# Latent attention's order rewritten on TensorE, ScalarE and VectorE

## What is computed

```python
h = xn @ w_down                                     # 1024 -> 256 + 128 + 32
c_q, c_kv, k_r = jnp.split(h, [256, 384], axis=-1)
q = (rms_norm(c_q, q_norm_g) @ w_uq).reshape(b, s, 16, 96)
q_n, q_r = q[..., :64], q[..., 64:]                 # q_r and k_r are rotated
kv = (rms_norm(c_kv, kv_norm_g) @ w_ukv).reshape(b, s, 16, 128)
k_n, v = kv[..., :64], kv[..., 64:]
logits = (q_n . k_n + q_r . k_r) * 96 ** -0.5
p = softmax(logits)
o = p . v
h = h + o @ w_out                                   # 1024 -> 1024
```

## Times and profile before

| | us |
|---|---|
| median of 3 runs | 1656.93 (1654.86 to 1660.21) |
| the profiled execution's own time | 1659.3 |
| its span | 1657.3 |
| TensorE busy in the span | 1632.1 (98%) |
| VectorE / ScalarE busy | 1050.7 (63%) / 852.4 (51%) |

### The profile page before, as it was taken

How to read it: one execution, slowest core, us unless ns; L and a number is a source line. 1 busy time by engine, 2 the same in 40 slices (tenths; PEclk the granted TensorE clock), 3 DMA queues, 4 the chain that set the end, 5 groups by cost and what they waited for, 6 DMA issues and landing times.

```text
span 1657.3 us, 24225 instructions
## 1 busy us (share of the span) xinstructions
PE 1632.1 (98%) x9542; PEld 1401.4 (85%) x9542; DVE 1050.7 (63%) x1197; ACT 852.4 (51%) x1078; POOL 51.1 (3%) x51
## 2 busy tenths in 40 slices
PE   8999999999999999999999999999999999999999
PEld 7878888757888888888897888888889999888887
DVE  6766565766665676667676666676667444566665
ACT  5654444665444464445675544564445444554443
POOL 2000000000000040000010000000000000000000
PEclk9999999989999999999999999999999999999999
DMA  9535554323554455554443555554545444445540
GB/s 368 193 126 194 200 202 181 124 89 111 220 203 181 180 189 200 188 192 157 148 166 141 208 183 195 184 201 183 202 178 192 176 154 166 166 153 203 203 177 26
DMA packets 42717, 294.24 MB, mean 178 GB/s; under 512 B 4736, under 2 KB 5040, under 8 KB 8592
## 3 DMA queue, kind: packets, MB, share of 16 engines
q1 hardware_dynamic: 39168, 281.04, 46.5%
q0 software_dynamic: 2752, 10.58, 1.8%
q10 hardware_dynamic: 720, 1.51, 0.2%
HBM read 289.96 MB, written 3.15 MB: 177 GB/s over the span
## 4 chain that ended last, share of the span: by engine, by line
PE 88%; DVE 6%; ACT 3%; issue 2%; DMA 1%; SPq 0%; DVEq 0%; ACTq 0%
PE ups L270 26%; PE accs L249 14%; PE accs L251 13%; PE accs L250 13%; PE ups L268 11%; DVE wlo L243 2%; PE ups L273 2%; ACT whi L239 1%; DVE h L652 1%; DMA raw<-weights 1%; PE ups L405 1%; PE ups L402 1%; PE ups L407 1%; PE ups L2290 1%; PE ups L448 1%
## 5 line engine op out<-in xcount | busy, mean ns | idle before, releaser
L243 DVE TENSOR_TENSOR wlo<-raw,whi 128x2048 fp32r<-128x2048 f32 x265 | 609.0, 2300 | 229.1 <-ACT whi L239 229.0
L270 PE MATMUL ups<-xhl,whi 128*128 128x512 f32 x1824 | 634.2, 396 | 0.0
L239 ACT CAST whi<-raw 128x2048 fp32r<-128x2048 f32 x265 | 505.2, 1909 | 79.2 <-PE accs L251 78.9
L268 PE MATMUL ups<-xhl,wlo 128*128 128x256 f32 x1596 | 445.0, 279 | 0.0
L270 PEld LDWEIGHTS ups<-xhl,whi 128*128 128x128 f32 x1824 | 331.0, 188 | 64.2
L268 PEld LDWEIGHTS ups<-xhl,wlo 128*128 128x128 f32 x1596 | 300.9, 189 | 10.1
L249 PE MATMUL accs<-whi,hidh 128*128 128x512 f32 x692 | 272.1, 393 | 0.0
L251 PE MATMUL accs<-whi,hidl 128*128 128x512 f32 x692 | 269.7, 390 | 0.0
L250 PE MATMUL accs<-wlo,hidh 128*128 128x512 f32 x692 | 269.5, 390 | 0.0
L249 PE MATMUL accs<-whi,xhl 128*128 128x256 f32 (+1 forms) x576 | 177.6, 308 | 1.6 <-DVE xhl L2140 1.6
L251 PE MATMUL accs<-whi,xhl 128*128 128x256 f32 (+1 forms) x576 | 172.1, 299 | 0.0
(11 more groups left out here) (263 smaller groups left out, 1614.1 us busy)
## 6 DMA issues: line engine op xcount, KB each, us to landing
raw<-weights SPq DMA_DIRECT2D x265, 1024.0 KB, 4.8
gain<-gains POOLq DMA_DIRECT2D x9, 512.0 KB, 3.8
rel_scratch<-sub_rstd POOLq DMA_DIRECT2D x1, 2048.0 KB, 17.4
big<-rel_scratch POOLq DMA_DIRECT2D x1, 1536.0 KB, 8.5
h<-x_in SPq DMA_DIRECT2D x2, 512.0 KB, 6.7
raw<-weights SPq DMA_DIRECT2D x2, 512.0 KB, 10.1
tabs<-consts POOLq DMA_DIRECT2D x1, 1024.0 KB, 7.2
gain<-gains ACTq DMA_DIRECT2D x1, 512.0 KB, 5.1
```

What stands on the lines that cost most here:

```text
L239: nc.scalar.copy(whi[:, m % SPLIT, :], raw[:, m % RAW, :]).then_inc(hi_ready, 1)
L243: nc.vector.tensor_tensor(wlo[:, m % SPLIT, :], raw[:, m % RAW, :], whi[:, m % SPLIT, :].bitcast(F32), ALU.subtract).then_inc(lo_ready, 1)
L268: nc.tensor.matmul(bank[:, 0:T], W(wlo, n, k, j * P, (j + 1) * P), xh[:, k, :], start=False, stop=False)
L270: mm = nc.tensor.matmul(bank, W(whi, n, k, j * P, (j + 1) * P), xhl[:, :, k, :], start=k == 0, stop=k == KC - 1)
```

## The change

The lists of the three engines are rewritten for the pairs of latent attention. No arithmetic, tile or transfer is added or dropped.

- TensorE: `vals(1, 0)` moves ahead of `scores(0)`, `keys(2)` and `vals(0, 1)` ahead of `turn(0)`, and so every later weight piece comes earlier; output pieces start in the fifth pair's round (behind `turn(7)`) where they began behind `turn(9)`. Of the third output slab three pieces run around `turn(15)` and `values(7)`, and `last_slabs` is entered with `begun=True`, behind them. Banks and counts are adapted (`c_taken` 7 for the second rotation).
- ScalarE: the split of `n_c + 4` runs ahead of `exps(0)`. The four splits of output slabs each come behind `turned_copy(2c)`: the first in pair 3, the others in pairs 4, 5 and 6.
- VectorE: `split_low` runs only behind `back(2c+1)`: for `n_co` in pair 3 (behind `back(7)`), and for the others in pairs 5, 6 and 7. `v_copy(0, 1)` runs behind `back(3)`.

The diff, cut to its core (every changed line; unchanged lines left out):

```diff
@@ -299,12 +299,15 @@
-def last_slabs(pe, n, f0, f1, q, ready=None):
-    pe.wait_ge(lo_ready, n + 1)
-    project_out(n, *f0, blocks=(0,))
-    project_out(n, *f0, blocks=(1,), halves=(0,))
+def last_slabs(pe, n, f0, f1, q, ready=None, between=None, begun=False):
+    if not begun:
+        pe.wait_ge(lo_ready, n + 1)
+        project_out(n, *f0, blocks=(0,))
+        if between:
+            between()
+        project_out(n, *f0, blocks=(1,), halves=(0,))
     pe.wait_ge(lo_ready, n + 2)
@@ -1309,7 +1312,7 @@
...
     def query_turn(s, bank):
-        pe.wait_ge(S("c_taken"), (1, 6)[s])
+        pe.wait_ge(S("c_taken"), (1, 7)[s])
         nc.tensor.matmul(bank, rotc, q_ropes, start=True, stop=True).then_inc(S("c_qrot"), 1)
@@ -1371,81 +1374,87 @@
...
     vals(0, 0, accs[:, 2, :]).then_inc(S("c_q"), 1)
+    pe.wait_ge(S("c_taken"), 2)
+    vals(1, 0, accs[:, 3, :]).then_inc(S("c_q"), 1)
     pe.wait_ge(S("c_taken"), 3)
...
     scores(0)
-    vals(1, 0, accs[:, 3, :]).then_inc(S("c_q"), 1)
     pe.wait_ge(S("c_taken"), 4)
     keys(1, accs[:, 0, :]).then_inc(S("c_q"), 1)
+    keys(2, accs[:, 1, :]).then_inc(S("c_q"), 1)
+    pe.wait_ge(S("c_v"), 1)
+    vals(0, 1, accs[:, 2, :]).then_inc(S("c_q"), 1)
     turn(0)
...
     pe.wait_ge(lo_ready, n_c + 5)
-    queries(4, 2, accs[:, 1, :]).then_inc(S("c_q"), 1)
     pe.wait_ge(S("c_v"), 2)
+    queries(4, 2, accs[:, 3, :]).then_inc(S("c_q"), 1)
     values(0)
-    queries(4, 0, accs[:, 2, :]).then_inc(S("c_q"), 1)
+    pe.wait_ge(S("c_taken"), 5)
+    queries(4, 0, accs[:, 0, :]).then_inc(S("c_q"), 1)
     turn(2)
-    pe.wait_ge(S("c_taken"), 5)
     scores(2)
     turn(3)
-    keys(2, accs[:, 3, :]).then_inc(S("c_q"), 1)
+    pe.wait_ge(S("c_v"), 3)
+    keys(3, accs[:, 2, :]).then_inc(S("c_q"), 1)
     values(1)
-    query_turn(1, accs[:, 0, :])
+    query_turn(1, accs[:, 1, :])
     turn(4)
...
     turn(5)
-    keys(3, accs[:, 1, :]).then_inc(S("c_q"), 1)
+    vals(1, 1, accs[:, 3, :]).then_inc(slab_used, 1)
     values(2)
-    pe.wait_ge(S("c_taken"), 7)
-    vals(0, 1, accs[:, 2, :]).then_inc(S("c_q"), 1)
+    pe.wait_ge(S("c_taken"), 8)
+    queries(4, 1, accs[:, 0, :]).then_inc(slab_used, 1)
     turn(6)
-    pe.wait_ge(S("c_taken"), 8)
     pe.wait_ge(S("c_qrope"), 2)
...
     turn(7)
-    vals(1, 1, accs[:, 3, :]).then_inc(slab_used, 1)
+    pe.wait_ge(lo_ready, n_co + 1)
+    pe.wait_ge(S("c_taken"), 10)
+    pe.wait_ge(S("att_o_low"), C_BASE // 2 + 2)
+    out_piece(0, 0, 0)
     values(3)
-    queries(4, 1, accs[:, 0, :]).then_inc(slab_used, 1)
+    out_piece(0, 0, 1)
     turn(8)
...
     turn(9)
-    pe.wait_ge(S("c_taken"), 10)
-    pe.wait_ge(lo_ready, n_co + 1)
-    pe.wait_ge(S("att_o_low"), C_BASE // 2 + 2)
-    out_piece(0, 0, 0)
     pe.wait_ge(S("c_v"), 4)
+    out_piece(0, 1, 0)
     values(4)
-    out_piece(0, 0, 1)
+    out_piece(0, 1, 1).then_inc(slab_used, 1)
     turn(10)
...
     turn(11)
-    out_piece(0, 1, 0)
-    values(5)
-    out_piece(0, 1, 1).then_inc(slab_used, 1)
-    turn(12)
-    scores(7)
-    turn(13)
     pe.wait_ge(lo_ready, n_co + 2)
...
     out_piece(1, 0, 0)
+    values(5)
     out_piece(1, 0, 1)
+    turn(12)
+    scores(7)
+    turn(13)
+    out_piece(1, 1, 0)
     values(6)
+    out_piece(1, 1, 1).then_inc(slab_used, 1)
     turn(14)
-    out_piece(1, 1, 0)
+    pe.wait_ge(lo_ready, n_co + 3)
+    pe.wait_ge(S("att_o_low"), C_BASE // 2 + 6)
+    out_piece(2, 0, 0)
     turn(15)
-    out_piece(1, 1, 1).then_inc(slab_used, 1)
+    out_piece(2, 0, 1)
     values(7)
-    pe.wait_ge(S("att_o_low"), C_BASE // 2 + 6)
-    last_slabs(pe, n_co + 2, features(4), features(6), 3,
+    out_piece(2, 1, 0)
+    last_slabs(pe, n_co + 2, features(4), features(6), 3, begun=True,
                ready=lambda: pe.wait_ge(S("att_o_low"), C_BASE // 2 + 8))
@@ -1518,69 +1527,51 @@
...
     heads(qc, 2, accs[:, 0, :])
+    split_high(act, n_c + 4)
     exps(0)
     exps(1)
-    split_high(act, n_c + 4)
-    turned_copy(0)
...
     heads(kc, 2, accs[:, 0, :])
+    turned_copy(0)
...
     act.wait_ge(S("c_q"), 7)
+    heads(kc, 4, accs[:, 1, :])
+    o_high(0)
+    act.wait_ge(S("c_q"), 9)
     act.wait_ge(S("c_qrope"), 1)
-    ropes(accs[:, 1, :])
-    o_high(0)
-    act.wait_ge(S("c_q"), 8)
-    heads(qc, 4, accs[:, 2, :])
+    ropes(accs[:, 3, :])
     turned_copy(2)
...
     exps(5)
-    act.wait_ge(S("c_q"), 9)
-    heads(kc, 4, accs[:, 3, :])
     o_high(1)
+    turned_copy(4)
+    act.wait_ge(S("c_q"), 10)
+    heads(qc, 4, accs[:, 0, :])
     split_high(act, n_co)
-    turned_copy(4)
...
     exps(7)
-    act.wait_ge(S("c_q"), 10)
-    heads(kc, 6, accs[:, 1, :])
     o_high(2)
...
-    turned_copy(7)
-    exps(8)
-    exps(9)
-    o_high(3)
+    act.wait_ge(S("c_q"), 11)
+    heads(kc, 6, accs[:, 2, :])
     act.wait_ge(slab_used, n_c + 5)
     heads(qc, 6, accs[:, 0, :])
-    split_high(act, n_co + 1)
-    turned_copy(8)
-    turned_copy(9)
-    exps(10)
-    exps(11)
-    o_high(4)
-    split_high(act, n_co + 2)
-    turned_copy(10)
-    turned_copy(11)
-    exps(12)
-    exps(13)
-    o_high(5)
-    split_high(act, n_co + 3)
-    turned_copy(12)
-    turned_copy(13)
-    exps(14)
-    exps(15)
-    o_high(6)
-    turned_copy(14)
+    for c in range(4, 8):
+        turned_copy(2 * c - 1)
+        exps(2 * c)
+        exps(2 * c + 1)
+        o_high(c - 1)
+        turned_copy(2 * c)
+        if c < 7:
+            split_high(act, n_co + c - 3)
     turned_copy(15)
@@ -1594,7 +1585,7 @@
...
     nc.gpsimd.tensor_tensor(kr_cos, kr_rows, cosC, ALU.mult).then_inc(S("c_cos"), 1)
-    pool.wait_ge(S("c_taken"), 6)
+    pool.wait_ge(S("c_taken"), 7)
     nc.gpsimd.tensor_tensor(q_cos, wide_q, wide_cos, ALU.mult).then_inc(S("c_cos"), 1)
@@ -1686,22 +1677,22 @@
...
     back(3)
+    dve.wait_ge(S("c_q"), 8)
+    v_copy(0, 1, accs[:, 2, :])
...
     back(5)
-    query_rope(1, accs[:, 0, :])
-    split_low(dve, n_co)
+    query_rope(1, accs[:, 1, :])
...
     back(7)
-    dve.wait_ge(S("c_q"), 11)
-    v_copy(0, 1, accs[:, 2, :])
+    split_low(dve, n_co)
@@ -1710,29 +1701,15 @@
...
     v_copy(1, 1, accs[:, 3, :])
-    split_low(dve, n_co + 1)
-    front(10)
-    front(11)
-    back(10)
-    o_low(4)
-    back(11)
-    split_low(dve, n_co + 2)
-    front(12)
-    front(13)
-    back(12)
-    o_low(5)
-    back(13)
-    split_low(dve, n_co + 3)
-    front(14)
-    front(15)
-    back(14)
-    o_low(6)
-    back(15)
+    for c in range(5, 8):
+        front(2 * c)
+        front(2 * c + 1)
+        back(2 * c)
+        o_low(c - 1)
+        back(2 * c + 1)
+        split_low(dve, n_co + c - 4)
     o_low(7)
```

More of the change, by code:

```diff
@@ L1429, in c_tensor @@
             turn(11)
-            out_piece(0, 1, 0)
+            pe.wait_ge(lo_ready, n_co + 2)
+            pe.wait_ge(S("att_o_low"), C_BASE // 2 + 4)
+            out_piece(1, 0, 0)
             values(5)
-            out_piece(0, 1, 1).then_inc(slab_used, 1)
+            out_piece(1, 0, 1)
             turn(12)
```

## The result

The changed kernel takes 1648.31 us (median of 6 runs, 1648.17 to 1650.7), against 1656.22 for the kernel before (6 runs, 1654.86 to 1660.21). The medians lie 7.9 us apart. The ratio taken over all these runs is 0.9949 (95% interval 0.9938 to 0.9960), which is 8.4 us of 1656.22: 0.5% faster. The forecast was 1650.4.

What follows compares the result with a forecast made beforehand. TensorE, busy 1632.1 of 1657.3 us, was taken as the bound. Attention terms 7.70 + 6.37 + 7.05 + 30.40 + 11.78 + 0.2 gave 63.5 against 72.42, so 8.9 less than 1659.3: 1650.4 us, range 1648.0 to 1654.9.

Steps and rivals of the forecast that it cites:

- The stretches: Attention from `turn(0)` through turns 2, 4, 6 and 14 to the norm's transposes, put at 63.5 us against 72.42.
- Its covers: TensorE work hiding other engines' latency: 3.93 against 3.02 us at `turn(6)`, 0.4 slack before output, 1.39 against 1.0 at last slab.
- The addition: Residual addition behind VectorE's split of the MLP's first slab, at the attention's end: claimed to start 0.2 us late.
- 4.4 us of the 8.9: Part of the 8.9 us gain put down to TensorE's low clock in the attention pairs no longer occurring.
- rival 2: The median run had no fall of clock in the attention, so only 4.5 us come off: 1652.4; chance 0.17.
- Rival 3: The clock falls all the same somewhere in the attention pairs, costing 4.4 us: 1654.8; chance 0.14.
- 2.9 from waits: Part of the 8.9 us gain claimed from TensorE's waits in the attention being removed: 2.9 us.
- 1.8 from work moved ahead of `turn(0)`: `keys(2)` and `vals(0, 1)` moved into TensorE's idle time ahead of `turn(0)`, claimed to gain about 1.8 us.
- The new order ends at the same 1650.4 from either: Whole kernel: claimed that executions of before with or without the fall of clock, 1659.3 or 1654.9, both become 1650.4 us.
- 1 to 1.5 us: Second low-clock stretch at 810, untouched by the change, may be missing in a median run; counted only in the range.
- A wait of 1.49 there [...] passed at a mean clock of 1.00: Evidence that the clock stays up: the old 1.49 us wait ahead of `turn(0)` had no fall in the profile.
- Rival 5: Slower: clock falls at the wait ahead of `turn(0)` and returns only near 353, costing 18 us: 1668; chance 0.03.

Runs made afterwards that it cites:

- experiment 9: Changed kernel with TensorE's output pieces back in their old places, weight pieces and splits left as changed: 1650.66 us, ratio 0.9961 to the kernel before.
- experiment 5: Kernel before with matmuls on zeros filling TensorE's waits ahead of `turn(0)` and `turn(6)`, order untouched: 1653.88 us, ratio 0.9982.
- 2: Kernel before with only VectorE's `split_low(n_co)` moved from ahead of `front(6)` to behind `back(7)`: 1652.96 us, ratio 0.9977.
- 8: Kernel before with only ScalarE's split of `n_c + 4` moved ahead of `exps(0)`: 1657.15 us, ratio 1.0005.
- experiment 1: The changed kernel run again, nothing altered: 1648.48 us, ratio 0.9949 to the kernel before.
- experiment 3: Kernel before with VectorE's `split_low(n_co)` behind `back(7)` and ScalarE's split of `n_c + 4` ahead of `exps(0)`, TensorE's list untouched: 1652.97 us, ratio 0.9970.
- experiment 6: Changed kernel with `keys(2)` and `vals(0, 1)` behind `turn(0)` instead of ahead of it: 1651.30 us, ratio 0.9967 to the kernel before.
- experiment 4: Changed kernel with VectorE's `split_low(n_co)` put back ahead of `front(6)`: 1650.77 us, ratio 0.9964 to the kernel before.

## Where the prediction was right, and where it went wrong

**The schedule.** The stretches were put at 7.70, 6.37, 7.05, 30.40 and 11.78 + 0.2 us, and are 7.68, 6.36, 6.97, 30.15 and 11.86. The sum, 63.5, is 63.02. The round is 7.54 and not 7.60. The old even turn started 0.05 us behind the end of its divisions (371.56 against 370.89 + 0.62), where the new one starts 1.25 us behind (365.64 against 363.77 + 0.62), so the old round probably still held a small wait for them. ScalarE's split of `n_co` stands in pair 2's list, behind `turned_copy(4)`, and not in pair 3 as the section on the change says; that is the pair ahead of VectorE's half, as the forecast took it.

**Its covers.** `turn(6)`, `out_piece(0, 0, 0)` and the last slab do not wait, as argued, though the slack of 0.4 ahead of the first output piece is 0.2 (VectorE's split ends at 353.81, the piece starts at 354.03). The addition begins as VectorE's split ends, also as argued, and the transposes wait 0.2.

**The clock.** The forecast gave 4.4 us of the 8.9 to it. Filling the waits of the kernel before, and nothing else, gave 4.55 in the stage and 3.9 in the median of executions. So rival 2 (no fall in the median run) is wrong. Rival 3 (the clock falls all the same) is wrong in both profiled executions of the changed kernel. In no trace does a fall begin in a round of the attention with waits of 0.2 us and less, and in experiment 9 a round with waits of 0.68 and 0.87 holds 1.00 too. The Trainium skill ("TensorE: Matmul & The Clock Gate", "A second HAM failure mode: psum-queue depth-cycling") tells of a kernel in which frequent short idle times, as it goes round PSUM banks, make the clock swing, and gives no length for them; at the lengths seen here it is not borne out.

**Where the 9.4 us of the stage come from**, by the profiled executions:

| step | stage | us gained |
|---|---|---|
| kernel before | 72.42 | |
| its waits filled: the clock (experiment 5) | 67.87 | 4.55 |
| both splits moved, at full clock (estimate from 2 and 8) | 66.1 | 1.8 |
| weight pieces moved up, the lists of ScalarE and VectorE as in the change (9) | 64.51 | 1.6 |
| output pieces from the fifth pair | 63.02 | 1.5 |

The text's own account has 2.9 from waits and 1.8 from work moved ahead of `turn(0)`, less the 0.2 of the late addition, which its sentence leaves out (2.9 + 1.8 + 4.4 is 9.1 and not 8.9). That is 4.5 for the 4.85 that are not clock. It did not say that the edits need each other: VectorE's split moved alone gives 0.9 us at full clock (66.93 against 67.87), as it takes 1.95 off the way to `turn(6)` and hands 1.0 back behind it, and the weight pieces moved up leave a round empty unless output pieces fill it. The shares depend on the order in which the edits are made.

**The step that failed** is "The new order ends at the same 1650.4 from either". The 8.9 us were taken off the profiled execution, 1659.3, and the result was set as the median. The two profiled executions differ by 8.6, so that the gain itself was nearly right, but taken off the median of before, 1656.93, it gives 1648.0; measured was 1648.31. The profiled execution of before had, besides the fall in this stage, low clocks at the start and near 810, and so had the profiled one of the changed kernel; its typical execution has less of them (experiment 1: 2.4 us). The text put "1 to 1.5 us" of that into the range and not into the forecast. The term mis-sized is the way from the profiled execution to the median: 0 taken for the new order, 2.4 measured (1650.7 to 1648.31), the same 2.4 as before (1659.3 to 1656.93). As a gain on the median, 6.5 us were forecast, and 7.9 to 9.4 measured (the two comparisons; 8.4 by their ratio). The stage gave 0.5 us more than forecast, and the 0.8 us by which `turn(0)` came later in the profiled execution took that back in it. The bounds 1648.0 to 1654.9 were too high for the same reason; 1648.31 lies 0.3 above the lower one.

**Evidence that was weaker than said.** "A wait of 1.49 there [...] passed at a mean clock of 1.00" was one execution. Experiment 3 has a fall behind the same wait, one trace of the four that have this wait unfilled. Rival 5 (slower by a fall that lasts) rested on the same place, and what the falls showed is against it: none in a trace lasted over 10.2 us.

## What to carry to other kernels

On an engine that is busy for 98% of the span, a wait of 1.5 to 2.2 us cost its length here and, in some of the executions, a further 1.2 to 4.5 us as low clock behind it. So the first thing to try is to fill the longest waits with matmuls on zeros: if the median falls, the clock is a part of the bill, and the real order is worth writing. In a list written by hand a step moved alone moves the wait (here to `turn(8)`); lay out the next two rounds of each engine before moving one. And a forecast made against one profiled execution has to say which of its low clocks the median run has.

## What the runs showed of the hardware

- **At one and the same wait the clock falls in some executions and not in others.** In the attention's traces it fell behind 1.49 us in one of four (experiment 3; not before, 2, 8), behind 1.9 in both (before, 8), behind 2.2 in the one (6), and not behind 1.68 (4) or anything under 0.9. By the groups of times, of which one execution each was profiled, it fell in three of eight executions with 1.7 us (experiment 4) and in nine of twelve with 2.2 (experiment 6). The kernel before scatters over 8.8 us, for the most part for this reason (its waits filled, seven of eleven executions lie within 0.5 us), with mean clocks of 0.993 to 0.999. At the start too the clock differs between executions of one kernel: 0.83 and 0.66 from 8 to 18 us (experiment 1). The Trainium skill ("TensorE: Matmul & The Clock Gate", "What's actually happening") says of a kernel's start that the count of slow matmuls changes from run to run; these two traces agree.
- **How long a fall lasts differs too:** 3.4 us in experiment 6, 6.9 in experiment 3, 10.2 in the kernel before. The shortest had `keys` and `vals` behind the turn, with all rows in use, the longer ones the scores on 64 and 32 rows. That this is the cause is not shown.
- **GpSimd holds up VectorE's divisions.** In the changed kernel its multiplication for the second rotation starts at 337.46, together with `back(3)`, whose two divisions take 1.68 us where the others take 0.62:

```profile
337.46 1.27 POOL L1589 TENSOR_TENSOR big<-hid,tabs 128x512 f32<-128x512 f32 x1 [15.81 <-ACT hid L1472]
```

  In the kernel before the same multiplication starts earlier, at 336.69, and the divisions that meet only its last half take 0.94:

```profile
337.45 0.94 DVE L1630 TENSOR_SCALAR xn<-xn,rden 128x256 f32<-128x256 f32 x2
```

  In experiment 3 it ends before they start (338.58 against 339.04), and they take 0.62. It cost nothing, as `front(4)` waited for the scores anyway. The Trainium skill ("SBUF — State Buffer", "SBUF: two separate sides") describes a port pair that GpSimd and some VectorE instructions take in turn, the other standing still meanwhile. The rows fit that for the most part: the divisions take 1.06 us longer beside 1.27 of multiplication, which is itself not slowed.
